# Norm parameters spread by TensorE, and 36 expert rows summed on VectorE, in a two-layer decoder trunk

## The reference

```
for layer in range(2):
    x = layer_norm(DN_ALPHA * x + mixer(x, ...), ln1_g, ln1_b)
    x = layer_norm(DN_ALPHA * x + peer_ffn(x, ...), ln2_g, ln2_b)

def layer_norm(x, g, b):
    ... return (xf - mu) * lax.rsqrt(var + LN_EPS) * g + b

def peer_ffn(x, w_q, sub_k1, sub_k2, u_tab, v_tab):      # for each block of 128 tokens
    q = (xb @ w_q);  s1, s2 = scores of q's halves against 128 keys each, for 8 heads
    eid, gate = 16 best of 16 x 16 pairs, for each head       # 8 * 16 = 128 experts for a token
    act = gelu(einsum('td,thkd->thk', xb, u_tab[eid]))
    return einsum('thk,thkd->td', gate * act, v_tab[eid])
```

## Time and profile before

| what | value |
|---|---|
| times of 3 runs | 1778.16, 1781.21 (median), 1781.8 us |
| profiled execution | 1780.13 us, span 1777.7 us |
| TensorE busy | 1538.4 us (87%) |
| VectorE busy | 1062.2 us (60%) |
| ScalarE busy | 604.7 us (34%) |
| GpSimd busy | 576.6 us (32%) |
| DMA | 638.32 MB, mean 359 GB/s |

### The profile page before, as it was taken

How to read it: one execution, slowest core, us unless ns; L and a number is a source line. 1 busy time by engine, 2 the same in 40 slices (tenths; PEclk the granted TensorE clock), 3 DMA queues, 4 the chain that set the end, 5 groups by cost and what they waited for, 6 DMA issues and landing times.

```text
span 1777.7 us, 18617 instructions
## 1 busy us (share of the span) xinstructions
PE 1538.4 (87%) x6020; PEld 921.1 (52%) x6020; DVE 1062.2 (60%) x2499; ACT 604.7 (34%) x1759; POOL 576.6 (32%) x561
## 2 busy tenths in 40 slices
PE   8999988999877778998899978998999968777776
PEld 7779977764322225763456525663457523222222
DVE  1584634577888875334556447665556468874444
ACT  1434411233333333227532323346632323332222
POOL 2000000244444442233432442334432444443441
PEclk9999958999999999999999999999999999999999
DMA  6222003899999999999999999999999999999996
GB/s 250 96 74 93 1 1 111 342 411 427 426 427 427 426 427 422 427 426 427 427 424 425 421 427 425 427 426 427 427 382 426 397 426 427 427 427 427 427 427 275
DMA packets 92063, 638.32 MB, mean 359 GB/s; under 512 B 11072, under 2 KB 13120, under 8 KB 15424
## 3 DMA queue, kind: packets, MB, share of 16 engines
q0 software_dynamic: 73728, 536.90, 71.8%
q1 hardware_dynamic: 18240, 100.24, 14.4%
HBM read 636.05 MB, written 1.05 MB: 358 GB/s over the span
## 4 chain that ended last, share of the span: by engine, by line
PE 52%; DMA 34%; ACT 6%; DVE 6%; issue 3%; POOL 1%; ACTq 0%; SPq 0%; POOLq 0%; DVEq 0%
DMA arena<-l_peer_uv,arena 33%; PE psum L905 22%; PE psum L587 14%; PE psum L886 5%; DVE arena L1715 3%; PE psum L764 2%; PE psum L809 1%; PE psum L680 1%; PE psum L670 1%; PE psum L679 1%; ACT L1202 1%; POOL arena L554 1%; ACT arena L1207 1%; ACT early L1215 1%; ACT arena L1215 1%
## 5 line engine op out<-in xcount | busy, mean ns | idle before, releaser
L554 POOL DMA_INDIRECT arena<-l_peer_uv,arena x512 | 563.4, 1100 | 1089.3 <-PE psum L905 828.9
L1715 DVE CUSTOM_DVE_ANT_0 arena<-arena,xres 128x1024 f32<-128x1024 f32 x512 | 619.3, 1223 | 406.5 <-DMA arena<-l_peer_uv,arena 400.9
L905 PE MATMUL psum<-arena,early 128*128 128x512 f32 x1024 | 477.6, 611 | 99.8 <-ACT early L1215 96.4
L905 PE MATMUL psum<-arena 128*128 128x512 f32 x1024 | 474.5, 608 | 95.7 <-ACT arena L1215 92.2
L905 PEld LDWEIGHTS psum<-arena,early 128*128 128x128 f32 x1024 | 189.4, 193 | 359.5 <-issue 200.4
L905 PEld LDWEIGHTS psum<-arena 128*128 128x128 f32 x1024 | 189.1, 192 | 354.8 <-issue 210.4
L587 PE MATMUL psum<-xT,wring 128*128 128x128 f32 (+2 forms) x1856 | 295.9, 319 | 12.5 <-DMA wring<-l_w_in 8.2
L587 PEld LDWEIGHTS psum<-xT,wring 128*128 128x128 f32 (+1 forms) x1856 | 268.5, 191 | 51.6 <-issue 21.1
L1202 ACT ACTIVATE arena<-arena 128x2 f32<-128x2 f32 x256 | 52.0, 203 | 595.4 <-DVE arena L1715 595.1
L1030 ACT COPY arena<-psum 128x256 f32<-128x256 f32 (+2 forms) x138 | 62.5, 472 | 220.8 <-PE psum L587 117.3
L1207 ACT ACTIVATE arena<-arena 128x1 f32<-128x1 f32 x512 | 123.3, 287 | 23.8
(11 more groups left out here) (236 smaller groups left out, 1142.7 us busy)
## 6 DMA issues: line engine op xcount, KB each, us to landing
wring<-l_w_in SPq DMA_DIRECT2D x47, 1024.0 KB
wring<-l_peer_wq SPq DMA_DIRECT2D x24, 1024.0 KB
wring<-l_w_out SPq DMA_DIRECT2D x12, 1024.0 KB
arena<-l_peer_uv,arena POOLq DMA_INDIRECT x512
ln_par<-l_ln_g SPq DMA_DIRECT2D x6, 512.0 KB
ln_par<-l_ln_b SPq DMA_DIRECT2D x6, 512.0 KB
arena<-l_peer_keys SPq DMA_DIRECT2D x2, 1024.0 KB, 6.9
xT<-x_t SPq DMA_DIRECT2D x1, 1024.0 KB, 4.8
```

What stands on the lines that cost most here:

```text
L554: pool.indirect_dma_start(out=ring[:, g % RING, :], out_offset=None, in_=T[f"l{l}_peer_uv"], in_offset=bass.IndirectOffsetOnAxis(ap=eid[:, ...
L905: last = mm(self.ps[c], diag[k % DIAGS], ring[:, g % RING, D + c * 512:D + (c + 1) * 512], start=not self.begun, stop=True, skip_group_che ...
L1715: v.tensor_tensor_reduce(out=u, in0=u, in1=xres[:, self.b, :], scale=1.0, scalar=0.0, op0=ALU.mult, op1=ALU.add, accum_out=hid[:, self.b, ...
```

## The change

Two things change.

1. The gains and biases of the three later norms come as one table of 12 rows by 512 numbers (`ln_rows`, 24 KB), which SP loads once into partitions 0 to 11 of a tile that the mLSTM no longer needs. For each of the five reloads, TensorE multiplies a column of the identity matrix (12 rows, spread over 128 columns) with the table, which puts one row of the table on all 128 partitions of a bank, four times (`spread_ln`). ScalarE copies the four banks into `ln_par` (`take_ln`). The layer norm waits for ScalarE's copies in place of a DMA. The first norm keeps its two broadcast loads.
2. In blocks 1 and 2, VectorE sums the slots 11, 15, 19 and so on to 79: 18 of 128 rows in each.

```diff
 def on_vector(n, s):
 
-    return False
+    return n in (1, 2) and 8 <= s < 80 and s % 4 == 3
...
+LN_ROWS = [NORMS[e][0] - 1 for e in range(2, len(NORMS) - 1)]
...
+    plan += [("ln_row", 4)]
     for b in range(NB):
-        plan += [("experts", 2), ("x_turn", 2), ("fox_f", 1), ("fox_qk", 4), ("fox_v", 2), ("fox_og", 2), ("fox_rms", 4)]
+        plan += [("experts", 2), ("x_turn", 2), ("fox_f", 1), ("fox_qk", 4), ("fox_v", 2), ("fox_og", 2), ("fox_rms", 4),
+                 ("ln_row", 4)]
         plan += [(name, 1) for name, _ in attention_plan(b)]
         plan += [("o_turn", 2), ("mix_out", 2), ("x_turn", 2)] + [("peer_q", 1), ("peer_s", 1)] * GROUPS
+        plan += [("ln_row", 4)]
...
+        ln_rows = mr[0:12, 4:6, :].rearrange("p a n -> p (a n)")
...
             load_keys(0)
+            sp.dma_start(ln_rows, T["ln_rows"]).then_inc(S("ln_rows_loaded"), 16)
             load_strips(6 - WRING)
-            load_ln(2)
...
                 load_strips(17 - WRING * (b == 0))
-                load_ln(3 + 2 * b)
                 load_strips(4 + 8)
-                load_ln(4 + 2 * b)
...
+            def spread_ln(i):
+
+                pe.wait_ge(S("ln_rows_loaded"), 16)
+                for t in range(4):
+                    r = 4 * LN_ROWS[i] + t
+                    done(mm(claim(pe, "ln_row", 4 * i + t), ident[0:12, r:r + 1].to_broadcast([12, P]), ln_rows,
+                            start=True, stop=True), "ln_row")
...
                 ex.pairs(RMS_PAIRS)
+                spread_ln(1 + 2 * b)
                 pe.wait_ge(S("qk_normed"), 4 * (b + 1))
...
             ex.pairs(sum(later_pairs(g, i) for g in range(GROUPS) for i in range(8)))
+            spread_ln(0)
             ex.finish()
...
                 mixer1_tail(b, ex)
+                spread_ln(2 + 2 * b)
                 ex.finish()
...
+            def take_ln(i):
+
+                act.wait_ge(S("x_normed"), i + 2)
+                for t in range(4):
+                    taken(copy(ln_par[:, t // 2, t % 2 * 512:(t % 2 + 1) * 512], full(act, "ln_row", 4 * i + t)), "ln_row")
...
-                dve.wait_ge(S("ln_loaded"), 32 * NORM_LOADS[e])
+                if NORM_LOADS[e] == 1:
+                    dve.wait_ge(S("ln_loaded"), 32)
+                else:
+                    dve.wait_ge(S("ln_row_taken"), 4 * (NORM_LOADS[e] - 1))
```

More of the change, by code:

```diff
@@ L451, in _ @@
             sp.dma_start(xres[:], T["x"].rearrange("o (b p) d -> p (o b) d", p=P)).then_inc(S("x_loaded"), 16)
[L453 to L459, removed]
             def load_keys(l):
                 sp.dma_start(keyT, T[f"l{l}_peer_keys"]).then_inc(S("keys_loaded"), 16)
-            load_ln(0)
+            sp.dma_start(ln_par[:, 0, :], T["l0_ln1_g"].partition_broadcast(P)).then_inc(S("ln_loaded"), 16)
+            sp.dma_start(ln_par[:, 1, :], T["l0_ln1_b"].partition_broadcast(P)).then_inc(S("ln_loaded"), 16)
             load_strips(16 + WRING - 3)
@@ L1287, in mixer1 @@
                 ex.pairs(RMS_PAIRS)
+                take_ln(1 + 2 * b)
                 w = P * (b + 1)
@@ L1337, in _ @@
             gates(1, PAIRS, lambda g, i: ex.pairs(later_pairs(g, i)))
+            take_ln(0)
             ex.finish()
@@ L1344, in _ @@
                 mixer1_tail(b, ex)
+                take_ln(2 + 2 * b)
                 ex.finish()
@@ L1882 @@
         laid[f"l{l}_peer_keys"] = keys.reshape(2 * EH, NK, P).transpose(2, 0, 1)
+    laid["ln_rows"] = _np.stack([laid.pop(f"{norm}_{part}") for norm in ("l0_ln2", "l1_ln1", "l1_ln2") for part in "gb"]).reshape(12, 512)
     for w in ("l0_w_in", "l0_w_out", "l0_peer_wq", "l1_w_in", "l1_w_out", "l1_peer_wq"):
```

## The result

The change makes the kernel slower, by 0.6%. In 8 runs each, on the same chips, the changed kernel took 1791.05 us at the median (1784.71 to 1798.79), the kernel before 1780.88 (1778.16 to 1782.22). The ratio is 1.0064, with a 95% interval of 1.0047 to 1.0081. I had said 1763.4, in a range of 1756 to 1774. The profiled execution of the changed kernel took 1798.79 us (span 1796.4), the slowest of the eight, so its windows show where time is lost rather than how much on the median. Part of the scatter isn't the change's: in this execution the first gather started at 326.7 us against 323.3 before, in table_only's at 320.5, and up to there the programs differ in loads alone.

What follows compares the result with a forecast made beforehand. The prediction took full DMA engines (bytes over rate) to bound the kernel from 340 to 1758 us. Gains of 9.8 for loads and 6.9 for dips, 16.7 us, took 1780.13 to 1763.4, range 1756 to 1774.

Steps and rivals of the forecast that it cites:

- The full stretch: From 340 to 1758 us the DMA engines are full at 423 GB/s, so its length is bytes over rate.
- The loads that go: Four pairs of broadcast loads in the full stretch, 2.46 us each, gain 9.8 us; the first pair counts nothing.
- The spreading that comes: Five sets of 4 matmuls and ScalarE copies: 17.2 us of TensorE, nothing on the path (bounds 0 and 11.6).
- The other three stand where TensorE waits for gathers: The three spreading sets not ahead of attention fall where TensorE waits anyway; part of the cost of nothing.
- The 36 rows that move: Blocks 1 and 2: TensorE loses 61.9 us of work, VectorE's sums stay hidden, block 2 attention steps shorten to 8.6 us.
- the 6.9 us of dips: DMA time lost at 1302 to 1314 and 1398 to 1410 with TensorE late; all taken as gained (bounds 0 and 6.9).
- What it costs the ring: Moved rows hold ring slots longer, 5.0 rows in flight against 7.4: cost nothing (bounds 0 and 36 us).
- the held slot: Rival, 0.09: VectorE keeps ring slots so long that DMA runs dry; 22 us lost, 1785.
- TensorE costs more than the two dips: Rival, 0.11: all the missing DMA rate in the full stretch, 13.3 us, is TensorE's; 1757.0.
- The loads were hidden: Rival, 0.09: where TensorE paces, as at 1180 and 1380, removed bytes gain nothing; if all are such, 1780.
- Only the bytes count: Rival, 0.19: the dips at 1302 and 1398 stay or come back elsewhere, only 9.8 us gained; 1770.3.

Runs made afterwards that it cites:

- table_only: Changed kernel with no row moved to VectorE, the spread parameters alone: 1790.29 us, 1.0053 of the kernel before.
- no_reload: Kernel before without the five later pairs of parameter loads and nothing in their place: 1774.23 us, 0.9963 of the kernel before.
- full_rows: table_only with a table of 128 rows (the last 116 zero) and the whole identity column: 1783.13 us, 1.0015 of the kernel before.
- late_full: full_rows with the sets behind the tails moved on by eight pairs, on TensorE and ScalarE: 1777.73 us, 0.9996 of the kernel before.
- rows_strips: Kernel before, broadcast loads kept, VectorE summing only slots 11 to 39 (8 each in blocks 1 and 2): 1785.22 us, 1.0027.
- held_slots: Kernel before, all rows on TensorE; GpSimd also waits for the dot four slots later before reusing the slots in question: 1781.16 us, 1.0001.
- late_12: table_only (12 rows) with the sets behind the tails moved on by eight pairs: 1782.17 us, 1.0015 of the kernel before.
- filled: Changed kernel with two unread 128x512 matmuls on TensorE in place of each moved row: 1789.66 us, 1.0044 of the kernel before.
- rows_only: Kernel before with the 36 rows on VectorE and the broadcast loads kept: 1785.69 us, 1.0024 of the kernel before.

## Why the prediction was wrong

- *The full stretch* stood: without the reloads the kernel gains (no_reload), and bytes do bound most of it. *The loads that go* were over-sized: 9.8 us counted, 6.6 measured, with an interval that still reaches 9.8; the trace puts the loss in block 2, where TensorE is late.
- *The spreading that comes* is the step that failed. I priced a 12-row matmul by the expert matmul of the same columns, and that was right: 4.37 us for a set at a clock that fell within it, 3.60 with 128 rows. I gave it "cost on the path: nothing". The runs show that a set behind a tail stands where TensorE isn't waiting for gathers but catching up, and that TensorE goes on at half clock behind a set of 12 rows. The first is worth 5.4 us (full_rows to late_full, 3.4 by the ratios), the second 7.2 (table_only to full_rows, 6.8 by the ratios); with both, table_only is 16.1 us above no_reload. The 3.5 us (5.9 by the ratios) between no_reload and late_full aren't assigned. My upper bound for the whole spreading was 11.6.
- "The other three stand where TensorE waits for gathers" was wrong for the two behind the tails, and could have been checked. TensorE was busy 6 of 6 us in 1404 to 1410, and I had used this row for something else. The place of the last set is the stretch in which I had found TensorE late.
- *The 36 rows that move.* VectorE's price was nearly right: 0.69 us predicted for a half, 0.747 in the page after:

```profile
L1754 DVE SCALAR_TENSOR_TENSOR masks<-arena,masks 128x512 f32<-128x512 f32 x68 | 48.0, 747 | 0.0
```

  That a step of block 2's attention would shorten to 8.6 us was wrong: it stayed 10.3. I had added up TensorE's work where the step is a loop over VectorE and ScalarE, in which the moved rows lay beside a wait of 4.2 us (from VectorE's start on the scores to the diagonals). The earlier trace rows showed the step but not what it is made of; one timeline of a step would have. So the 6.9 us of dips had no cause to go. The four additions to the residual, priced at 2.8 us, I put nowhere on the path; two of them lie ahead of a norm for which TensorE waits (rows_strips). As for GpSimd, the new sums didn't lengthen its issues: 1078 ns at the mean after, 1100 before.
- *What it costs the ring:* nothing was right as far as held_slots tests it, which is a hold for the dots; the longer hold for the sums isn't priced alone. The rival *the held slot* had the right sign, but most of the loss comes with no row moved (table_only).
- *TensorE costs more than the two dips* isn't borne out. *The loads were hidden* seems right for the two pairs that it names (4.8 us more lost behind them), and wrong for all five: no_reload gains. *Only the bytes count* had it right that the dips stay, and it still left out the cost of the spreading.
- The halves, +9.4 us for the table and +4.3 for the rows (ratios 1.0053 and 1.0024 of 1780), come to a little more than the 11.4 of both; the intervals allow for a plain sum.
- From 1763.4 to the measured 1791.05: 3.2 us of loads that weren't gained, 6.9 of dips that stayed, 16.1 for the spreading, 0.8 from table_only to the change. That makes 1790.4. It is bookkeeping of what was measured in steps, and says only that the spreading is the largest step.

## What to carry to other kernels

A load replaced by TensorE's work isn't free because TensorE waits somewhere: put the work where the timeline shows it waiting, and look at the clock right behind it. Before moving work off an engine, lay out one step of the loop in order of time and see whether that work is in the loop or beside a wait; here the choice of the row within a group of four decided between 10.3 and 9.8 us a step, though alone it didn't shorten the kernel. And run the parts of a change alone: the part that I had taken for a sure gain was the one that lost.

## What the runs showed of the hardware

- TensorE's granted clock went from 1.00 to 0.50 while it was busy without a gap, in and behind four matmuls of 12 rows by 512 columns (table_only), and didn't with four of 128 rows (full_rows: 3.60 us for the pair that follows, against 6.37). It was back at 1.00 from 1010 on (0.72, 0.50, 0.50 and 0.57 in the four windows from 1002 to 1010). In the four traces with 12 rows (table_only, late_12, filled and the changed kernel) it fell at 15 of 20 sets, in full_rows and late_full, with 128 rows, at none of 10.
- In rows_only, with gaps of 2.1 us in the steps of token block 0's attention (the first at 825.02, behind a wait for ScalarE), the granted clock there was 0.93 where it had been 1.00.
